# The first normalisation of a two-block network: its scale vector as a row spread by TensorE, and the first weight rounded between the two blocks of rows

## What is computed

```python
def rms_norm(x, g):
    x32 = x.astype(jnp.float32)
    y = x32 * lax.rsqrt(jnp.mean(x32 * x32, axis=-1, keepdims=True) + EPS)
    return (y * g.astype(jnp.float32)).astype(x.dtype)
...
        xn = rms_norm(h, g_mix_pre[i])
        z = xn @ w_in[i]
        conf_ab, q, k, v, f_logit, sc_h, sc_b, sc_c, pool_v = jnp.split(z, SPLIT_IDX, axis=-1)
```

## Time and profile before

| | |
|---|---|
| time, median of 3 runs | 954.39 us (954.23 to 954.42) |
| profiled execution | 954.84 us, of which 953.0 us are the span of the profile |
| PE busy | 936.0 us, 98% of the span |
| PEld busy | 813.3 us, 85% |
| DVE busy | 680.7 us, 71% |
| ACT busy | 518.3 us, 54% |
| POOL busy | 91.5 us, 10% |
| chain that ended last | PE 80%, DVE 11%, ACT 5%, issue 2%, POOL 1%, DMA 1% |

### The profile page before, as it was taken

One profiled execution on the slowest core, in us unless ns is written; L12 is line 12 of the kernel. 1 busy time (PEld: TensorE's weight loads), 2 busy tenths in 40 slices (PEclk: granted clock), 3 DMA queues, 4 the chain that ended last, 5 costly groups with the idle time before them and its releaser, 6 DMA issues.

```text
span 953.0 us, 12969 instructions
## 1 busy us (share of the span) xinstructions
PE 936.0 (98%) x5245; PEld 813.3 (85%) x5245; DVE 680.7 (71%) x875; ACT 518.3 (54%) x711; POOL 91.5 (10%) x111
## 2 busy tenths in 40 slices
PE   8999999999999999999999999999999999999997
PEld 7998788888888798788888888889998788888885
DVE  5899857666667977866676666568989767666663
ACT  6887545444546566965544434468685445434432
POOL 2550200000011100100000000000233010000000
PEclk9999999999999999999999999999999999999999
DMA  9933666566535455146656565556423447656531
GB/s 290 342 128 125 203 210 212 193 204 195 203 133 199 131 167 177 45 133 221 219 179 194 182 199 177 176 158 218 135 90 111 133 144 255 219 177 191 182 113 44
DMA packets 106955, 166.94 MB, mean 175 GB/s; under 512 B 2896, under 2 KB 82848, under 8 KB 106768
## 3 DMA queue, kind: packets, MB, share of 16 engines
q1 hardware_dynamic: 104688, 158.23, 51.0%
q0 software_dynamic: 2208, 7.89, 2.3%
HBM read 165.06 MB, written 1.05 MB: 174 GB/s over the span
## 4 chain that ended last, share of the span: by engine, by line
PE 80%; DVE 11%; ACT 5%; issue 2%; POOL 1%; DMA 1%; DVEq 0%; ACTq 0%; POOLq 0%
PE ps L400 78%; DVE wl L1880 3%; PE ps L408 2%; DVE SC L2504 1%; ACT wh L1266 1%; DVE SC L1998 1%; DMA raw<-in_s_w_in 1%; DVE fs L2008 0%; ACT SC L1600 0%; POOL st L2708 0%; DMA h<-in_x 0%; ACT junk L1254 0%; ACT xhl L1277 0%; DVE xf L2566 0%; ACT SC L1775 0%
## 5 line engine op out<-in xcount | busy, mean ns | idle before, releaser
L1880 DVE TENSOR_TENSOR wl<-raw,wh 128x2048 fp32r<-128x2048 f32 (+2 forms) x146 | 329.1, 2259 | 142.1 <-ACT wh L1266 142.1
L1266 ACT ACTIVATE wh<-raw 128x2048 fp32r<-128x2048 f32 (+2 forms) x150 | 282.0, 1886 | 155.2 <-PE ps L400 141.8
L400 PE MATMUL ps<-xhl,wh 128*128 128x512 f32 (+1 forms) x1248 | 254.6, 350 | 0.3 <-ACT wh L1335 0.3
L400 PEld LDWEIGHTS ps<-xhl,wh 128*128 128x128 f32 x1248 | 199.2, 190 | 26.9 <-issue 0.7
L400 PE MATMUL ps<-wh,xhl 128*128 128x512 f32 (+3 forms) x800 | 190.5, 379 | 0.4 <-DVE xhl L1897 0.4
L400 PEld LDWEIGHTS ps<-wh,xhl 128*128 128x128 f32 x800 | 142.6, 188 | 25.7 <-DVE xhl L1897 0.8
L400 PEld LDWEIGHTS ps<-xhl,wl 128*128 128x128 f32 x1008 | 135.7, 191 | 7.5
L400 PE MATMUL ps<-xhl,wl 128*128 128x256 f32 x1008 | 140.6, 282 | 0.0
L400 PE MATMUL ps<-wl,xhl 128*128 128x512 f32 (+3 forms) x395 | 101.9, 379 | 2.0 <-DVE wl L1880 1.9
L400 PE MATMUL ps<-wh,fh 128*128 128x512 f32 x304 | 91.0, 392 | 0.3 <-DVE fl L2237 0.3
L400 PE MATMUL ps<-wh,fl 128*128 128x512 f32 x304 | 90.1, 389 | 0.0
(11 more groups left out here) (297 smaller groups left out, 820.4 us busy)
## 6 DMA issues: line engine op xcount, KB each, us to landing
raw<-in_ffn_gate SPq DMA_DIRECT2D x22, 1024.0 KB, 5.4
raw<-in_ffn_up SPq DMA_DIRECT2D x22, 1024.0 KB, 5.3
raw<-in_ffn_down SPq DMA_DIRECT2D x22, 1024.0 KB, 4.9
raw<-in_w_up SPq DMA_DIRECT2D x16, 1024.0 KB, 5.5
raw<-in_w_down SPq DMA_DIRECT2D x16, 1024.0 KB, 5.0
raw<-in_s_w_in SPq DMA_DIRECT2D x14, 1024.0 KB, 5.4
raw<-in_w_in SPq DMA_DIRECT2D x9, 1024.0 KB, 9.7
raw<-in_a_w_in SPq DMA_DIRECT2D x6, 1024.0 KB, 5.3
```

Of the source, the lines that this page charges most:

```text
L400: return e.matmul(o, a, b, start=start, stop=stop, skip_group_check=True)
L1266: e.activation(high_of(i), raw_of(i), ACT.Copy).then_inc(*up("act_high", i))
L1880: e.tensor_tensor(low_of(i), raw_of(i), high_of(i).bitcast(F32), ALU.subtract).then_inc(*up("dve_lo", i))
```

## The change

- SP loads `g_mix_pre` as one row of 4 KB into partition 0 of `rows`, between the two loads of `h`. POOL writes 128 ones beside it. PE multiplies the column of ones by the row, twice 512 columns, which puts the gain into all partitions of PSUM banks 5 and 6.
- DVE scales all four halves with 1/rms and gain in one instruction each, the gain read from PSUM. ACT no longer scales block 1, and `norm_columns` is gone; `xh` and `xl` are made from PSUM directly.
- DVE's mean of block 1 now stands between the two halves of block 0.
- ACT rounds the first half of slot 0 between the columns of block 0 and those of block 1.
- PE's first product is issued by output half and by half of the inner dimension, with a wait for each; 4 of the 13 warm-up calls are left.
- POOL's load of `g_mix_post` into `rows` waits until PE has read the gain.

```diff
@@ tensor
-                    e.wait_ge(*(at("act_hs", n, c) if (n, tb) == (0, 1) else at("dve_hs", n, tb, c)))
+                    e.wait_ge(*at("dve_hs", n, tb, c))
...
-                warm(6)
+                warm(2)
+                e.wait_ge(*at("dma_gain"))
+                for c in range(2):
+                    mm(ps[GAIN[c]][:, :], rows[0:1, 1, 0:128], rows[0:1, 0, HALF[c]], True, True).then_inc(*up("pe_gain", c))
                 e.wait_ge(*at("dma_ident"))
                 norm_turn(0, 0)
-                warm(2)
+                warm(1)
                 norm_turn(0, 1)
-                warm(5)
-                e.wait_ge(*at("act_xh", 0, 1, 1))
+                warm(1)
                 wH, wL = weight(S["a"])
...
+                def first(t, w, x, k0, start, stop):
+                    for k in range(k0, k0 + 4):
+                        d = mm(ps[(4, 2)[t]][:, 0:256], w[:, k, 128 * t:128 * t + 128], x[:, k, :], start and k == 0, stop and k == 7)
+                    return d
+
+                e.wait_ge(*at("act_first_high"))
+                for c in range(2):
+                    e.wait_ge(*at("act_xh", 0, 1, c))
+                    first(0, wH, xh, 4 * c, True, False)
+                for t in range(2):
+                    if t == 1:
+                        e.wait_ge(*at("act_high", 0))
+                        for c in range(2):
+                            first(1, wH, xh, 4 * c, True, False)
+                    for c in range(2):
+                        if t == 0:
+                            e.wait_ge(*at("dve_xl", 0, 1, c))
+                        first(t, wH, xl, 4 * c, False, False)
+                for t in range(2):
+                    e.wait_ge(*(halves_ready(S["a"]) if t else at("dve_first_low")))
+                    for c in range(2):
+                        d = first(t, wL, xh, 4 * c, False, True)
@@ scalar
-                e.wait_ge(*at("pool_rstd", "norm", 0, 1))
-                for c in range(2):
-                    e.activation(hs[:, 1, HALF[c]], h[:, 1, HALF[c]], ACT.Identity, scale=st[:, 5:6]).then_inc(*up("act_hs", 0, c))
                 norm_high(0, 0)
-                norm_high(0, 1)
                 e.wait_ge(*at("dma_raw0", 0))
                 for t in range(2):
+                    if t == 1:
+                        norm_high(0, 1)
@@ vector
-                    if n == 0:
-                        d = e.tensor_scalar(hs[:, tb, HALF[c]], h[:, tb, HALF[c]], st[:, 3 * tb + 2:3 * tb + 3], None, ALU.mult)
...
+                        e.wait_ge(*at("pe_gain", c))
+                        if (tb, c) == (0, 1):
+                            norm_mean(0, 1)
+                    g = grow[:, n % 2, HALF[c]] if n else ps[GAIN[c]][:, :]
+                    e.scalar_tensor_tensor(hs[:, tb, HALF[c]], h[:, tb, HALF[c]], st[:, 3 * tb + 2:3 * tb + 3], g,
+                                           ALU.mult, ALU.mult).then_inc(*up("dve_hs", n, tb, c))
...
-                norm_mean(0, 1)
-                for tb in range(2):
-                    norm_columns(tb)
+                norm_scale(0, 1)
@@ gpsimd
+            e.memset(rows[0:1, 1, 0:128], 1.0).then_inc(*up("pool_zero", "ones"))
...
+            e.wait_ge(*at("pe_gain", 1))
             e.dma_start(rows[:, 0, :], D["g_mix_post"].partition_broadcast(128)).then_inc(*up("dma_row0", 0))
@@ sync
                 e.dma_start(h[:, tb, :], D["x"][tokens(tb), :]).then_inc(*up(f"dma_h{tb}"))
+                if tb == 0:
+                    e.dma_start(rows[0:1, 0, :], D["g_mix_pre"].unsqueeze(0)).then_inc(*up("dma_gain"))
```

More of the change, by code:

```diff
@@ L345, in place @@
             return slice(256 * k, 256 * k + 256)
+        GAIN = (5, 6)
         GAIN_ROW = [None, D["g_mlp_pre"], D["g_ple_pre"], *(D[f"norm_{k}_{l}"] for l in range(2) for k in ("mix", "ffn"))]
@@ L594, in first_mixer @@
                 wH, wL = weight(S["a"])
-                for n, (w, x) in enumerate(((wH, xh), (wH, xl), (wL, xh))):
-                    for t in range(2):
-                        if n == 0:
[L598 to L605, removed]
+                def first(t, w, x, k0, start, stop):
+                    for k in range(k0, k0 + 4):
+                        d = mm(ps[(4, 2)[t]][:, 0:256], w[:, k, 128 * t:128 * t + 128], x[:, k, :], start and k == 0, stop and k == 7)
+                    return d
@@ L1270, in norm_high @@
                 for c in range(2):
[L1271 to L1276, removed]
+                    e.wait_ge(*at("pe_turned", n, tb, c))
+                    x = ps[TURN[n][tb][c]][:, :].rearrange("p (k n) -> p k n", k=4)
                     e.activation(xh[:, 4 * c:4 * c + 4, tokens(tb)], x, ACT.Copy).then_inc(*up("act_xh", n, tb, c))
@@ L1923, in norm_rows @@
                 norm_scale(n, tb)
[L1925 to L1928, removed]
             def norm_low(n, tb):
@@ L1932, in norm_low @@
                     t, s = slice(4 * c, 4 * c + 4), tokens(tb)
-                    x = xf[:, t, s] if n == 0 else ps[TURN[n][tb][c]][:, :].rearrange("p (k n) -> p k n", k=4)
+                    x = ps[TURN[n][tb][c]][:, :].rearrange("p (k n) -> p k n", k=4)
                     e.wait_ge(*at("act_xh", n, tb, c))
@@ L2948 @@
     arrays = {"x": a["x"][0], "pT": np.ascontiguousarray(a["p"][0, 0].T), "prm": prm, "srow": srow, "cst": cst,
-              "g_mlp_pre": a["g_mlp_pre"][0], "g_ple_pre": a["g_ple_pre"][0], "band": band, "hmask": hm, "w_pool": a["w_pool"][0], "norm_final_2": a["norm_final_2"]}
+              "g_mix_pre": a["g_mix_pre"][0], "g_mlp_pre": a["g_mlp_pre"][0], "g_ple_pre": a["g_ple_pre"][0], "band": band, "hmask": hm, "w_pool": a["w_pool"][0], "norm_final_2": a["norm_final_2"]}
     for n in ("w_in", "w_conf_pw", "w_out", "w_up", "w_down", "w_ple_gate", "w_ple_proj", "g_mix_post", "g_mlp_post",
```

## The result

The changed kernel takes 956.13 us in the median (954.87 to 957.84, 21 runs), the kernel before beside it 954.61 (954.17 to 955.60, 21 runs): a ratio of 1.0015 with a 95% interval of 1.0010 to 1.0021. So the change costs 1.5 us; the forecast was a gain of 1.0, and 956.1 lies above the range. The spread matters too: 3.0 us between the fastest and the slowest run against 1.4 before.

What follows compares the result with a forecast made beforehand. ACT's queue was taken to set PE's first product at 12.99 us, then PE, and DVE with the weight stream. DVE's 1.15 or 0.45 plus 0.25 gave 1.4 or 0.7, taken as 1.0: 953.4 us, 8-in-10 range 952.5 to 954.8.

Steps and rivals of the forecast that it cites:

- The second half of `h`, `prm` and the weights issued 0.43 us later: Loads behind the gain row at the start: costed at nothing, covered by the DMA's own queue at 305 GB/s.
- inside the two ends: Second half waits for the second gain product until 7.4 to 8.1 anyway; mean or power 0.4 us late fits inside.
- I take the same price, since I count columns.: PE's gain products: one partition assumed to cost the same as 128; 512 columns take 1.7 us slow, 0.86 quick.
- my slow case: PE's pace stays slow at the start: second gain product done at 8.1, first product at 12.05, sum 0.7 us.
- The rule named against the forecast: PE's clock is throttled by default and activity releases it; by that the slow case is expected, 0.7 us or less.
- Row, DVE, ACT.: Start steps: row lands at 4.5 (3.8 to 5.6), DVE scalings take 0.70, ACT loses 1.33 us, high parts 594 ns.
- the term that counts: DVE's first half of the weight's low part starts at 12.4 or 13.1 against 13.55: 1.15 or 0.45 us earlier.
- The other term of the sum: DVE's wait of 0.25 us for PE at 60.11 goes as well, since PE leads by more than DVE.
- It moves the load of slot 3, the waits at 22.63 and 40.43, POOL's loads.: DVE's earlier low half moves the weight stream: slot 3 near 21.8, slot 6 near 39.6, DVE's stretch from 41.6.
- the signs of being wrong: Gain products after 5, first real records 0.43 apart, slot 6 still at 40.4, start's move not found at 60 and 90.
- The rivals: PE's lead passed on whole, 952.7 us, chance 0.12; nothing gained, 954.4, 0.18; slower by a low clock, 955.5, 0.10.
- The one on the other side: Slower: PE's first products start at the low clock; if it lasts to 17 us, 955.5 us; chance 0.10.

Runs made afterwards that it cites:

- the hold: Edit used in several runs: POOL's further loads (3.5 MB) wait for ACT's high part of slot 4 instead of slot 3.
- e5: Changed kernel with the gain row's 4 KB load issued on ACT's queue ahead of everything: 955.81 us, ratio 1.0009 to the kernel before.
- e11: Changed kernel with the gain row on ACT's queue and POOL's loads after slot 4: 954.09 us, ratio 0.9994 to the kernel before.
- e7: Changed kernel with POOL's further loads waiting for slot 4 instead of slot 3: 955.05 us, ratio 1.0003 to the kernel before.
- e12: Kernel before with only POOL's loads moved behind slot 4: 954.22 us, ratio 0.9995.
- e14: Kernel before with the 4 KB row between the halves of `h` and POOL's loads after slot 4: 954.75 us, ratio 1.0004.
- e4: Kernel before with only the gain row's 4 KB load added between the halves of `h`, read by nobody: 956.18 us, ratio 1.0019.
- e8: Kernel before with its first six warm-up calls multiplying one partition instead of 128: 956.68 us, ratio 1.0023.
- e9: Changed kernel with the row on ACT's queue and gain products over 128 partitions, 127 of them zeros: 956.67 us, ratio 1.0022 to the kernel before.
- e10: Changed kernel with row on ACT's queue, gain products over 128 partitions (127 zeros), POOL's loads after slot 4: 955.10 us, ratio 1.0003 to the kernel before.
- e13: Changed kernel with row on ACT's queue, POOL's loads after slot 4, one warm-up call moved behind the gain products: 954.10 us, ratio 0.9994 to before.
- e6: Changed kernel with 28 idle instructions on TensorE ahead of the first product: 955.45 us, ratio 1.0012 to the kernel before.
- e3: Kernel before with 28 fewer TensorE instructions, 13 warm-up calls of 256 columns made into 6 of 512: 955.59 us, ratio 1.0007.
- e15: Kernel before with six warm-up calls of 512 columns for thirteen of 256, and POOL's loads after slot 4: 954.33 us, ratio 0.9996.

## Why the prediction was wrong, by its own steps

- **"The second half of `h`, `prm` and the weights issued 0.43 us later", costed at nothing.** This is the first step that failed, by its size. The issue is only 0.35 us later, but the landing was up to 1.5 us late. In the profiled execution after, `prm` held up POOL's first power (6.81, not 6.20), and the first scaling went from 6.79 to 7.40. Even so the price stayed there "inside the two ends", as forecast: e5 and e11, with the half early, begin the other three scalings at 8.17, this one at 8.19, and come to DVE's first low half at 13.68 and 13.49, this one at 13.54. Where the half comes later nothing covers it: squared from 7.21 in e7, it has the first scaling at 8.11 and the first low half at 14.40. Its time varies: in the profiled executions with the row on SyncE's queue the second half was squared from 5.99, 6.36, 6.44, 6.53, 7.21 and 7.32; without it from 5.69 to 6.05. The row's place is worth 0.5 in the kernel before (e12, e14) and 1.0 in the changed one (e7 to e11), both with the hold; with no hold 1.5 (e4) and 0.3 (e5), the last not clear of the spread. Why a landing can be 1.5 us late isn't shown.
- **"I take the same price, since I count columns."** The product's own time was right: 3.78 us for both, done at 8.0, my slow case 8.1. What I left out is that the same clock runs the transposes behind it: I took 0.8 us from the scaled half to ACT's first high part in both cases. Block 0's eight transposes took 1.94 instead of 1.06, and ACT's first high part came at 9.41, not 8.3; 0.6 of that is the late first scaling. I also let the transposes start when the first half was scaled, at 7.5, though the second gain product holds TensorE until 8.0: in e5 the half is scaled at 7.55 and the first transpose starts at 7.93. e8 shows in the kernel before that such products leave the pace slow, and its price there, 2.2 us. What it costs inside the changed kernel was not isolated: e9 and e10 started too late, and e13 left block 0's transposes slow. The rule named against the forecast, the slow case, is what came; but DVE's lead fell short of that end too.
- **Row, DVE, ACT.** The row was there for 4.22, within the bounds; three scalings in 2.16 are 0.72 each, I had 0.70; ACT's high parts take 595 ns. The order of work was as foreseen. The lead at DVE's first low half, "the term that counts", was 0.01 us instead of 0.45 to 1.15; with the early `h` it was 0.04 in e11 and 0.22 in e13 (13.49 and 13.31, against 13.53 in e12). The other term of the sum, the wait of 0.25 us for PE at 60.11, did go, and won nothing, since DVE itself came to its next low part at 61.58, not at 60.65.
- **"It moves the load of slot 3, the waits at 22.63 and 40.43, POOL's loads."** The second step that failed, and about half of the loss: with the hold in both kernels the change costs 0.8 (955.05 against 954.22), without it 1.5. Slot 3 came at 21.45, near my 21.8, but not because DVE was early: the code load of TensorE had moved off it. The earlier slot 3 released POOL's 3.5 MB at 23.66 instead of 24.84, which I had listed as a gain. They took the DMA engines from slot 5 (waited for until 30.96) and slot 6 (41.74, my figure 39.6). I had shifted the whole stream by a constant, where the release of one queue against the demands of another decides. Of the signs of being wrong that I had named, two came: slot 6 no earlier than 40.4, and a lead of the first product that isn't found again at 60 and 90 us.
- **The rivals.** None was this. The one on the other side put the loss on products at the low clock; the clock had risen by 11.91, before the first product at 12.44.

With the row on ACT's queue and POOL's loads held the changed kernel (954.09) stands beside the kernel before with the same hold (954.22), a difference inside the runs' spread: the change itself, well placed, is worth nothing that can be told apart here. So the loss of 1.5 us is some 0.7 of collision (1.1 for the hold here, 0.4 in the kernel before) and 1.0 of the row's place; with both taken away 0.1 is left the other way, inside the spread. The slow pace of the transposes is the likely reason, not shown inside this kernel, why the forecast gain of 1.0 is missing as well. Both lie some 0.5 us below the kernel before, with intervals that reach 1.0003. e11 and e13 have the lowest medians (954.09 and 954.10) and the fastest single runs, but neither beats before beyond its interval.

## What to carry to other kernels

- A tiny load put between two large ones on a busy queue isn't free; look at who waits for the next one, and put it on a queue that is idle.
- Before you count an earlier release as a gain, ask what else hangs on it. An engine that is freed earlier may start traffic that takes the bandwidth from the load that the chain waits for.
- Taking instructions away, idle warm-ups too, shifts TensorE's loads of code against the weights; look for the instruction queue among the DMAs, and test with idle instructions in their place.

## What the runs showed of the hardware that I had not expected

- After products over one partition TensorE was still at its slow pace: 12 records of 256 columns in 5.48 us and the eight transposes behind them in 1.97, against 1.06 in the kernel before (e8). The column of granted clock reads 1.00 there too; the spacing of the records shows it.
- A load of 4 KB between two of 512 KB made the second up to 1.5 us late (e4), though its issue came only 0.35 us later.
- One 16 KB packet of code takes one DMA engine for 1.05 us, and 28 instructions more or less on TensorE moved it from one weight slot to another. The median moved by 0.7 and 0.9 us (e6, e3), neither clear of the spread, and by 0.1 where POOL's loads came later (e15).
